# Expert weights in 32 KB rows and 4 MB transfers from the ninth expert on, with every expert's features renumbered to suit

## The reference, cut to what matters

```
h = rmsnorm(x, g_ffn_norm)
logits = h @ w_router + b_router            # top 4 of 32 experts for each token
for each expert e, for the tokens that chose it:
    gu   = h @ w_gate_up[e] + b_gate_up[e]  # w_gate_up[e]: 1024 x 2048, 8 MB
    gate = minimum(gu[:, :1024], 7);  up = clip(gu[:, 1024:], -7, 7)
    act  = gate * sigmoid(1.702 * gate) * (up + 1)
    y   += g * (act @ w_down[e] + b_down[e])   # w_down[e]: 1024 x 1024, 4 MB
```

## Time and profile before

| | us |
|---|---|
| median of three runs | 1517.38 |
| the profiled execution | 1516.06 |
| its span, first to last instruction | 1514.2 |
| PE busy | 1443.0 |
| DVE busy | 351.8 |
| ACT busy | 217.4 |

### The profile page before, as it was taken

The page is one execution under the profiler, slowest core; times in us unless marked ns, Lnnn a source line. Parts: engine busy times, 40 slices in busy tenths (PEclk is TensorE's granted clock), DMA queues, the critical chain, the costliest instruction groups (busy, mean ns, idle before and its releaser), DMA issues.

```text
span 1514.2 us, 17900 instructions
## 1 busy us (share of the span) xinstructions
PE 1443.0 (95%) x7236; PEld 774.4 (51%) x7236; DVE 351.8 (23%) x873; ACT 217.4 (14%) x404; POOL 21.9 (1%) x14
## 2 busy tenths in 40 slices
PE   7999999999999999999999999999699997999999
PEld 5655444444343334334334433433398865888843
DVE  5535411121121111112111111211423453002310
ACT  1331011111011011101101110110213342100000
POOL 3200000000000000000000000000000000000000
PEclk9998999999999999999999999999899998999999
DMA  9999889999999999999999999999943222444400
GB/s 336 348 417 409 334 345 428 429 428 428 428 427 429 428 429 429 429 428 428 428 427 429 428 429 429 429 429 428 373 153 121 84 84 84 139 157 149 139 0 28
DMA packets 82717, 497.00 MB, mean 328 GB/s; under 512 B 6253, under 2 KB 47930, under 8 KB 54682
## 3 DMA queue, kind: packets, MB, share of 16 engines
q1 hardware_dynamic: 82076, 495.46, 80.6%
q10 hardware_dynamic: 606, 1.06, 0.2%
HBM read 495.44 MB, written 1.05 MB: 328 GB/s over the span
## 4 chain that ended last, share of the span: by engine, by line
PE 54%; DMA 41%; DVE 3%; issue 1%; ACT 1%; SPq 0%; DVEq 0%; ACTq 0%
DMA ring<-in_w_gate_up_dram 40%; PE PS L876 13%; PE PS L1202 10%; PE PS L997 6%; PE PS L1209 5%; PE PS L902 4%; PE PS L861 2%; PE PS L767 2%; PE PS L614 2%; PE PS L719 2%; PE PS L1081 1%; PE PS L597 1%; PE PS L910 1%; DMA ring<-in_w_ada_dram 1%; PE PS L722 0%
## 5 line engine op out<-in xcount | busy, mean ns | idle before, releaser
L876 PE MATMUL PS<-ring,work 128*64 128x512 f32 x2016 | 449.4, 596 | 29.6 <-DMA ring<-in_w_gate_up_dram 28.5
L876 PEld LDWEIGHTS PS<-ring,work 128*64 128x64 f32 x2016 | 139.1, 137 | 322.5 <-issue 246.1
L902 PE MATMUL PS<-ring,work 128*64 128x512 f32 x1024 | 225.1, 592 | 0.0
L1898 DVE TENSOR_SCALAR work<-PS 128x512 f32<-128x512 f32 x32 | 22.1, 691 | 641.2 <-PE PS L876 641.2
L1202 PE MATMUL PS<-cols,ring 128*128 128x256 f32 x704 | 154.8, 383 | 2.1 <-issue 2.1
L1202 PEld LDWEIGHTS PS<-cols,ring 128*128 128x128 f32 x704 | 135.5, 193 | 21.8 <-DVE cols L1602 2.5
L902 PEld LDWEIGHTS PS<-ring,work 128*64 128x64 f32 x1024 | 71.8, 137 | 131.9 <-issue 129.5
L861 PE MATMUL PS<-work,rows 128*128 128x64 f32 x1056 | 128.5, 276 | 0.4 <-DVE work L1876 0.4
L861 PEld LDWEIGHTS PS<-work,rows 128*128 128x128 f32 x1056 | 126.6, 196 | 1.3 <-DVE work L1876 1.3
L997 PE MATMUL PS<-ring,cols 128*128 128x240 f32 (+1 forms) x448 | 95.5, 371 | 2.1 <-DVE cols L1602 2.1
L997 PEld LDWEIGHTS PS<-ring,cols 128*128 128x128 f32 x448 | 85.2, 193 | 8.3 <-DVE cols L1602 2.5
(11 more groups left out here) (297 smaller groups left out, 930.9 us busy)
## 6 DMA issues: line engine op xcount, KB each, us to landing
ring<-in_w_gate_up_dram SPq DMA_DIRECT2D x126, 2048.0 KB, 24.3
ring<-in_w_down_dram SPq DMA_DIRECT2D x64, 2048.0 KB, 20.3
ring<-in_w_ada_dram SPq DMA_DIRECT2D x24, 1024.0 KB, 17.4
ring<-in_w_gate_up_dram SPq DMA_DIRECT2D x22, 1024.0 KB, 5.1
ring<-in_w_in_dram SPq DMA_DIRECT2D x13, 960.0 KB, 10.8
ring<-in_w_down_dram SPq DMA_DIRECT2D x11, 1024.0 KB, 4.9
ring<-in_w_out_dram SPq DMA_DIRECT2D x8, 1024.0 KB, 9.9
ring<-in_w_in_dram SPq DMA_DIRECT2D x3, 1024.0 KB, 12.2
```

The source lines that it names most:

```text
L876: mm = pe.matmul(bank(b)[CAP * h:CAP * (h + 1), :], xg[:, k, :], w[:, b * FE + h * 512:b * FE + (h + 1) * 512], start=False, stop=(k == KD ...
L902: mm = pe.matmul(bank(3)[CAP * h:CAP * (h + 1), :], lhs, w[:, (f % 2) * D + h * 512:(f % 2) * D + (h + 1) * 512], start=False, stop=(f == 7))
```

## The change

From the ninth expert (e = 8, `FINE`) to the last but one, an expert comes in three transfers of four slots, 4 MB each, whose rows are 32 KB. To make this possible the features are renumbered: four neighbouring rows of `w_gate_up` and eight of `w_down` belong to one partition. The first eight experts and the last one (`LAST`) use the same numbering, but load two slots at a time: a 16 KB half of each 32 KB row. The slots are shifted (`SKEW`) so that the four-slot units line up with the ring. Gate and up columns for the upper and lower 64 rows of a bank are now interleaved in groups of four (`half_columns`), so the moving operand of L876 is read as runs of four float32 (16 bytes) at every 32 bytes, and that of the bias matmul L870 as runs of four bfloat16.

```diff
+UNIT = 4
+FINE, LAST = 8, EXPERTS - 1
+SKEW = -N_MOE % SLOTS
...
-        gu_dram = ins["w_gate_up"][0].rearrange("e (j p k) n -> (e j) p (k n)", p=P, k=2)
-        dn_dram = ins["w_down"][0].rearrange("e (s p k) n -> (e s) p (k n)", p=P, k=4)
+        gu_dram = ins["w_gate_up"][0].rearrange("e (j p k) n -> (e j) p (k n)", p=P, k=4)
+        dn_dram = ins["w_down"][0].rearrange("e (p k) n -> e p (k n)", p=P)
+        def slots_at(c, n):
+            return ring[:, c:c + n, :].rearrange("p a b -> p (a b)")
+        def unit_source(e, c, n):
+            src = gu_dram[bass.ds(e * 2 + c // UNIT, 1), :, :] if c < KD else dn_dram[bass.ds(e, 1), :, :]
+            return src.rearrange("o p n -> (o p) n")[:, (c % UNIT) * SLOT:(c % UNIT + n) * SLOT]
         def ffn_order(row):
-            return row.rearrange("p (j q k) -> p j k q", j=4, k=2)
+            return row.rearrange("p (j q k) -> p j k q", j=2, k=4)
...
-            with sp.Fori(3, EXPERTS) as e:
+            with sp.Fori(3, FINE) as e:
                 for c in range(0, SLOTS, 2):
-                    load_pair(e, c, e * SLOTS + (N_MOE + c + 2 - SLOTS))
+                    load_slots(e, c, 2, e * SLOTS + (N_MOE + c + 2 - SLOTS))
+            with sp.Fori(FINE, LAST) as e:
+                for c in range(0, SLOTS, UNIT):
+                    load_slots(e, c, UNIT, e * SLOTS + (N_MOE + c + UNIT - SLOTS))
+            for c in range(0, SLOTS, 2):
+                load_slots(LAST, c, 2, LAST * SLOTS + (N_MOE + c + 2 - SLOTS))
...
-            for k in range(2):
-                mm = pe.transpose(bank(6)[:, GFFN_AT + 4 * k:GFFN_AT + 4 * k + 4],
-                                  gffn.rearrange("j (p k) -> j p k", k=2)[:, :, k], ident[0:4, 0:4])
+            for k in range(4):
+                mm = pe.transpose(bank(6)[:, GFFN_AT + 2 * k:GFFN_AT + 2 * k + 2],
+                                  gffn.rearrange("j (p k) -> j p k", k=4)[:, :, k], ident[0:2, 0:2])
...
+            def half_columns(w, b, h):
+                return w[:, b * FE:(b + 1) * FE].rearrange("p (q k) -> p q k", k=8)[:, :, 4 * h:4 * h + 4]
...
-                                           w[:, b * FE + h * 512:b * FE + (h + 1) * 512],
+                            mm = pe.matmul(bank(b)[CAP * h:CAP * (h + 1), :], xg[:, k, :], half_columns(w, b, h),
...
-                        if c % 2 == 0:
-                            pe.wait_ge(landed[s], expert_landings(e, c))
+                        if c % step == 0:
+                            pe.wait_ge(landed[s], expert_landings(e, c, first))
...
-            with pe.Fori(2, EXPERTS) as e:
-                expert(e)
+            with pe.Fori(2, FINE) as e:
+                expert(e, 2, 2)
+            with pe.Fori(FINE, LAST) as e:
+                expert(e, FINE, UNIT)
+            expert(LAST, LAST, 2)
...
-                    dst, src = dst.rearrange("p (j k q) -> p j k q", j=4, k=2), ffn_order(src)
+                    dst, src = dst.rearrange("p (j k q) -> p j k q", j=2, k=4), ffn_order(src)
```

More of the change, by code:

```diff
@@ L104 @@
 N_MOE = N_OUT1 + 4 + len(ADA_CHUNKS) - ADA_MID
-assert N_MOE % 2 == 0
 LEAD = 4
+UNIT = 4
+FINE, LAST = 8, EXPERTS - 1
+SKEW = -N_MOE % SLOTS
 N_IN2 = N_MOE + EXPERTS * SLOTS
@@ L127, in slot_of, with step_of @@
 def slot_of(n):
-    return (n if n < N_MOE else n - LEAD) % SLOTS
+    return (n + SKEW - (0 if n < N_MOE else LEAD)) % SLOTS
 def expert_slot(e, i):
-    return (N_MOE + i - (0 if isinstance(e, int) and e == 0 else LEAD)) % SLOTS
+    return (i - (0 if isinstance(e, int) and e == 0 else LEAD)) % SLOTS
+def step_of(e):
+    return 2 if e < FINE or e == LAST else UNIT
 LANDINGS = {}
@@ L142 @@
 for _e in range(EXPERTS):
-    for _i in range(LEAD if _e == 1 else 0, SLOTS, 2):
+    for _i in range(LEAD if _e == 1 else 0, SLOTS, step_of(_e)):
         _count[expert_slot(_e, _i)] += 1
@@ L148, with expert_landings @@
     LANDINGS[_n] = _count[slot_of(_n)]
-def expert_landings(e, i):
+def expert_landings(e, i, first):
     if isinstance(e, int):
         return 16 * LANDINGS[e, i]
-    return e * 16 + 16 * (LANDINGS[3, i] - 3)
+    return e * 16 + 16 * (LANDINGS[first, i] - first)
 VEC_ROWS = {}
@@ L244, in two_blocks @@
         vec = sb("vec", [NVEC, P])
-        gffn = sb("gffn", [4, 2 * P])
+        gffn = sb("gffn", [2, 4 * P])
         vcol = sb("vcol", [P, NVEC + KD])
@@ L491, in _ @@
                               "bada_in")
-            load_small(gffn[:, :], ins["g_ffn_norm"].rearrange("o (j p) -> (o j) p", j=4), "vec2_in")
+            load_small(gffn[:, :], ins["g_ffn_norm"].rearrange("o (j p) -> (o j) p", j=2), "vec2_in")
             for name, (at, n) in VEC_ROWS.items():
@@ L509, in _ @@
                 if n == SLOTS + 2:
-                    load_small(router[:, :, :].rearrange("p (j k) e -> p j (k e)", k=2), ins["w_router"][0].rearrange("(j p k) e -> p j (k e)", p=P, k=2), "router_in")
+                    load_small(router[:, :, :].rearrange("p (j k) e -> p j (k e)", k=4),
+                               ins["w_router"][0].rearrange("(j p k) e -> p j (k e)", p=P, k=4), "router_in")
                     load_small(brouter[:, :], ins["b_router"][0].partition_broadcast(P), "brouter_in")
@@ L516, in _, with load_slots @@
                     load_small(bias14[:, 10:14], ins["ml_i_bias_2"][0].partition_broadcast(P), "bias14_in")
-            def load_pair(e, c, used):
+            def load_slots(e, c, n, used):
                 s = expert_slot(e, c)
                 sp.wait_ge(chunk_used, used)
-                sp.dma_start(pair_of(s), pair_source(e, c)).then_inc(landed[s], 16)
+                sp.dma_start(slots_at(s, n), unit_source(e, c, n)).then_inc(landed[s], 16)
             def load_lead(dst, lo, wait, n):
                 sp.wait_ge(sig[wait], n)
-                row = gu_dram[4 + lo // (2 * SLOT), :, lo % (2 * SLOT):][:, 0:dst.shape[1]]
-                sp.dma_start(dst, row).then_inc(sig["lead_in"], 16)
-            load_pair(0, 0, N_MOE + 2 - SLOTS)
+                sp.dma_start(dst, gu_dram[2, :, lo:lo + dst.shape[1]]).then_inc(sig["lead_in"], 16)
+            load_slots(0, 0, 2, N_MOE + 2 - SLOTS)
             load_lead(lead_a, 0, "scores_done", HEADS)
@@ L530, in _ @@
             for c in range(2, SLOTS, 2):
-                load_pair(0, c, N_MOE + c + 2 - SLOTS)
+                load_slots(0, c, 2, N_MOE + c + 2 - SLOTS)
             load_lead(lead_c, 3 * SLOT, "parts_done", 1)
             for c in range(LEAD, SLOTS, 2):
-                load_pair(1, c, N_MOE + c + 2 - LEAD)
+                load_slots(1, c, 2, N_MOE + c + 2 - LEAD)
             for c in range(0, SLOTS, 2):
-                load_pair(2, c, N_MOE + SLOTS + c + 2 - (LEAD if c < LEAD else 0))
-            with sp.Fori(3, EXPERTS) as e:
+                load_slots(2, c, 2, N_MOE + SLOTS + c + 2 - (LEAD if c < LEAD else 0))
+            with sp.Fori(3, FINE) as e:
                 for c in range(0, SLOTS, 2):
-                    load_pair(e, c, e * SLOTS + (N_MOE + c + 2 - SLOTS))
+                    load_slots(e, c, 2, e * SLOTS + (N_MOE + c + 2 - SLOTS))
[4 more added lines that the diff above has]
+                load_slots(LAST, c, 2, LAST * SLOTS + (N_MOE + c + 2 - SLOTS))
             sp.wait_ge(sig["lists_ready"], 1)
@@ L547, in _ @@
                         e = sp.value_load(lists[0:1, bass.ds(j, 1)], min_val=0, max_val=EXPERTS - 1)
-                        for c in range(0, SLOTS, 2):
-                            sp.dma_start(pair_of(c), pair_source(e, c)).then_inc(sig["o_loaded"], 16)
+                        for c in range(0, SLOTS, UNIT):
+                            sp.dma_start(slots_at(c, UNIT), unit_source(e, c, UNIT)).then_inc(sig["o_loaded"], 16)
                         sp.wait_ge(sig["o_down"], j + 1)
@@ L870, in moe_gate_up @@
                         pe.matmul(bank(b)[CAP * h:CAP * (h + 1), :], sel_b[:, :],
-                                  bias_b[:, b * FE + h * 512:b * FE + (h + 1) * 512], start=True, stop=False)
+                                  half_columns(bias_b, b, h), start=True, stop=False)
                 for k in range(KD):
@@ L919, in _, with expert, weights @@
             pe.wait_ge(sig["bias_split"], 2)
-            def expert(e):
-                def weights(first):
+            def expert(e, first, step):
+                def weights(c0):
                     def get(i):
-                        c = first + i
+                        c = c0 + i
                         if isinstance(e, int) and e == 1 and c < LEAD:
@@ L950, in expert @@
                 moe_down(weights(KD), lambda mm, s: mm.then_inc(chunk_used, 1))
-            expert(0)
-            expert(1)
-            with pe.Fori(2, EXPERTS) as e:
-                expert(e)
+            expert(0, 0, 2)
+            expert(1, 1, 2)
+            with pe.Fori(2, FINE) as e:
[3 more added lines that the diff above has]
+            expert(LAST, LAST, 2)
             pe.wait_ge(sig["yb_ready"], EXPERTS + 1)
@@ L968, in _ @@
```

(6 more changed lines are left out.)

7 lines of the change are left out of this document (removed).

## The result

The changed kernel takes 1520.67 us (median of 20 runs, 1517.72 to 1523.89), the kernel before 1516.51 us in 20 runs beside it. The ratio is 1.0023, 95% interval 1.0015 to 1.0032: 0.23% slower, where 0.24% faster was forecast. The medians lie 4.2 us apart. The time lies 0.7 us beyond the stated range. The profiled execution has a span of 1520.7 us, 6.5 us over the one before.

The account below looks back on a forecast made before the run. Experts from the ninth on were taken as paced by bytes at 428.5 GB/s. Terms -5.4 + 1.7 + 0.1 = -3.6 us gave 1513.8 us (0.24% less) from 1517.4, range 1508.5 to 1520.

Parts of the forecast that it names:

- the small edits: VectorE's wider step, two more transposes, loops in more pieces: taken as 0.1 us in all; VectorE at most 1.5 us.
- Term 1: Expert weight transfers: 32 KB rows in 4 MB transfers save 0.24 us per expert, 5.4 us over 22.67 experts.
- rival (a): Expert transfers: larger fixed part, saving 0.30 to 0.45 us per expert, total 1509 to 1512.4 us; chance 22%.
- the sum: Whole kernel: -5.4 + 1.7 + 0.1 = -3.6 us, giving 1513.8 us on the median.
- (b): Expert transfers: hardware handles 32 KB rows as 16 KB pieces, period stays 29.36 us, about +1.8 us, 1519.2; chance 13%.
- (d): Expert transfers: large rows or new spacing move slower; at 420 GB/s +15 us, 1533; chance 8%.
- the timetable: Expert stage: each four-slot transfer is issued at least 8 us before its turn, so no gap and no cost.
- Term 2: PE's wait moves from slot 6 to slot 4: new 3.3 us idle at ninth expert, 1.7 us lost at the end.
- Term 3: Gate/up matmuls L876 read 16-byte runs at 32-byte steps: taken as no cost, judged from L888's transposes.
- rival (c): Strided read slows PE in the gate/up matmuls; at a third, +108 us, about 1625; chance 5%.

Follow-up runs that it names:

- one_loop: Changed kernel's transfers, but TensorE runs experts 2 to 31 in one loop, SyncE raising the second pair's semaphore; ratios to the kernel before 0.9998, on repeat 0.9991.
- no_spare_path: Changed kernel with TensorE's never-entered branch for crowded experts deleted; ratio to the kernel before 0.9990.
- one_loop_fine4: Kernel with TensorE's single loop and large transfers, the latter starting at the fifth expert instead of the ninth; ratio to the kernel before 0.9990.

## Why the prediction was wrong

**The step that failed** is the one among the small edits: "The loops in more pieces: PE entered its present loop without idle time (the windows of 160 to 240 us show it busy throughout), so nothing." Entering a loop is not the only place where the position of code matters. Behind the experts PE jumps over the spare path for crowded experts. With the code of one or two experts more ahead of it the jump leaves PE idle for about 5 us (4.68 to 5.11 us in six kernels), without that code for nothing (four kernels and the one before). The page shows a trace of it: the instruction queue q8 moved 24 packets of 16 KB in the kernels without the extra code and 26 or 27 with it. In the changed kernel's packet records this queue moves nothing between 391 and 1052 us, and then one packet at 1081.8, inside the idle, and one at 1087.7 us. In all six kernels with the idle such a packet lies inside it, and PE goes on 2.6 to 2.7 us after it began. In the kernel before there is one at 1082.6 us, when PE has already gone on, and the kernel without the spare path has one at 1080.4 us and no idle. That PE waited for the code at the target is the reading that fits all these runs. That it is the fetch, and why 5 us, is argued from the packets, not shown. No run varied the length of the jump but to take it away, or the code ahead by less than one expert's.

**The idle has a tail.** From the first matmul behind it to the end of the span, the profiles without the idle took 434.2 to 435.5 us, those with it 434.2 to 436.3. The granted clock fell to 0.50 in this place in every kernel, for 17 us in those without the idle and for 20.5 to 23.9 us in the six with it. The changed kernel had the longest stretch to the end, and its first 64 instructions of the next projection took 16.13 us against 15.05. That difference makes my estimate of the tail, up to 1 us; single profiles don't resolve it.

**Term 1, the rate: right.** Forecast 0.24 us per expert, measured 29.365 - 29.144 = 0.22, so the fixed part is not the larger one of rival (a). That the fixed part belongs to the row and not to the transfer is new: the sum had left this open, and the run with 16 KB rows in 4 MB settled it. Rivals (b) and (d) are out. The stream stayed unbroken, as the timetable said.

**Term 2, the edges: right.** 1.7 us forecast. The stage gained 3.32 us where 22.67 x 0.22 = 5.0 us were on offer, so 1.7 were lost; the run with 16 KB rows in large transfers shows 1.8. In the last expert PE waits for no weight, as said. In the ninth it waited 0.33 and 2.62 us, together 2.95 where one wait of 3.3 was forecast: slot 0 was late as well.

**Term 3: right in its result, and wrong in its evidence.** L891 takes 13.73 us for 64 instructions, as L876 did: groups of four at a moving operand cost nothing, and rival (c) is out. But L888 could not show that, since it has no strided moving operand. In a transpose the data is the weight. The changed kernel's transposes of the gains show it by their sizes, 2x128 of data loaded and 2x2 of the identity moving:

```profile
L700 PEld LDWEIGHTS PS<-cst,gffn x4: 190/212/212, 65.3 to 65.6; 2*128 2x128 f32 x4
L700 PE MATMUL PS<-cst,gffn x4: 254/254/275, 65.3 to 65.7; 2*128 2x2 f32 x4
```

As a row on weight loads L888 was read too mildly. Its 215 ns were set against 162, the median of a mixture from 138 to 231 ns. The contiguous transposes L883 of the same stage are the nearer neighbour, and their loads take 140 ns in the kernel before:

```profile
L883 PEld LDWEIGHTS PS<-cst,work x64: 137/140/143, 168.9 to 1065.8; 128*128 128x128 f32 x64
```

So the step of 16 bytes already cost a weight load half its time again, in the trace that the prediction had. In the gather it went from 192 to 330 ns. Had the change needed strided weights there, taking nothing from L888 would have let an 11% loss pass. The expectation of that run leans on the same reading.

**The small edits, VectorE's part: mis-sized.** What the prediction and the earlier trace rows call a strided write is a strided read: VectorE reads the features at a step and writes them in order. The read in the earlier trace rows has a step of 8 bytes, the new one 16. Taken as nothing with a bound of 1.5 us, the cost was 1.16 - 0.75 = 0.41 us, twice. On PE it arrived in part: the transposes behind it start as soon as before, and the last one ends 0.44 us later. The Trainium skill (Advanced Engine Details and Errata, Memory Cachelines) asks for two hits in a line of 16 bytes, which a float32 step of 8 bytes gives and one of 16 does not. By that rule, the trace agrees on both sides: 0.75 us against 1.16. The rule had been weighed for PE and not for VectorE. On TensorE's weight loads it is less clear: the two of the gains before, at a step of 8 bytes, took 191 and 212 ns, and the four now, at 16 bytes, take 190 to 212. The gains' transposes took 0.64 us instead of 0.40, but there the chain of waits runs through VectorE. From the PE group ahead of them (L677, now L688) to the PE work behind them it takes 7.06 us, as it took 7.07 before. So they cost nothing, for 0.1 taken.

**The sum again**, with what was measured: -3.3 (the stage) + 5.0 (the jump) + 0.4 (VectorE) + up to 1 (the tail) = +2.1 to +3.1 us. Timed: 0.23% of 1516.5, +3.5 us, with an interval of 2.3 to 4.9. Without the jump and its tail it is -2.9 us, in place of the forecast -3.6. The four timings of kernels with large rows and no idle (one_loop twice, no_spare_path, one_loop_fine4) give -0.3, -1.4, -1.5 and -1.5 us, with intervals of about 2 us on either side. All four lie on the same side of -2.9, so part of the stage's gain seems not to reach the whole time; no run says where it goes.

## What to carry to other kernels

A change to transfers that also splits a loop or writes out a copy is two changes: compare with a kernel that has the new code and the old transfers. A program that jumps over rarely used code paid some 5 us for it here or nothing, by the amount of code ahead, so look for an idle named "issue" behind every loop and branch. Before a row is used as a bound, make sure which operand of the instruction is the strided one, whether the step in bytes is the same, and whether the row that it is compared with is of one kind or a mixture.

## What the runs showed of the hardware

- Transfers of 4 MB in rows of 32 KB ran at 432 GB/s; in rows of 16 KB the rate was 428.5, whether a transfer had 2 or 4 MB.
- VectorE's float32 tensor_scalar of 1024 columns: 0.75 us with reads contiguous or at 8 bytes, 1.16 at 16 bytes, 1.22 with writes at 512 bytes.
- TensorE's float32 weight load of 128 columns: in the gather 192 ns contiguous and 330 ns at 16 bytes, in transposes 140 and 212. A moving operand in runs of 16 bytes at 32 bytes: no difference in 64 instructions.
- Slower weight loads can cost more than themselves: with PE busy throughout, the granted clock fell to 0.50 within the slow gather in every expert, 0.85 over a period, and the down matmuls took 9.11 us instead of 7.04.
- A jump over code that is not run: no idle on TensorE in the kernel before and in four others, 4.68 to 5.11 us in the six with more code ahead of it.
